# A two-block layer kernel: constants, first modulation, first normalisation, token turn and first projection made one stage

## The reference, cut to what matters

```
mod = silu(c) @ w_ada + b_ada                     # c: 1 x 1024, w_ada: 1024 x 6144
sh_m, sc_m, gt_m, sh_f, sc_f, gt_f = split(mod, 6)
u = layer_norm(x) * (1 + sc_m) + sh_m             # per token over 1024 columns
proj = u @ w_in                                   # w_in: 1024 x 2568
q, k, v, f_logit, xb, gb = split(proj, ...)       # 512 columns each; f_logit 8
...
```

## Time and profile before

| | |
|---|---|
| median of 3 runs | 2962.95 us |
| the profiled execution, own time | 2974.41 us |
| its span | 2972.7 us |
| PE / DVE / ACT / POOL busy over the span | 85% / 75% / 53% / 11% |
| end of the five stages in question | 211.98 us |
| first matmul of the projection | 74.12 us |

### The profile page before, as it was taken

One profiled execution on the slowest core, in us unless ns is written; L12 is line 12 of the kernel. 1 busy time (PEld: TensorE's weight loads), 2 busy tenths in 40 slices (PEclk: granted clock), 3 DMA queues, 4 the chain that ended last, 5 costly groups with the idle time before them and its releaser, 6 DMA issues. The chain is left out here.

```text
span 2972.7 us, 35763 instructions
## 1 busy us (share of the span) xinstructions
PE 2524.2 (85%) x12008; PEld 2035.5 (68%) x12008; DVE 2228.7 (75%) x2169; ACT 1572.1 (53%) x1443; POOL 337.3 (11%) x271
## 2 busy tenths in 40 slices
PE   2979774899982999778893999999999999999981
PEld 1862654677772888667773777777777777777761
DVE  4557874788775431678646899999999999999984
ACT  2214621676654431546421677777767777777760
POOL 1110100232320000000000011111111111111110
PEclk9989885999995999889985999999999999999995
DMA  5855222899974241010213899999999999999984
GB/s 185 284 192 195 26 105 111 325 350 367 372 269 159 89 127 48 1 67 19 71 73 128 323 367 367 365 365 368 366 364 364 369 362 370 364 367 366 367 306 163
DMA packets 247345, 731.59 MB, mean 246 GB/s; under 512 B 29388, under 2 KB 57307, under 8 KB 245023
## 3 DMA queue, kind: packets, MB, share of 16 engines
q1 hardware_dynamic: 223172, 645.64, 60.1%
q0 software_dynamic: 21792, 80.75, 7.1%
q10 hardware_dynamic: 2304, 4.20, 0.4%
HBM read 692.73 MB, written 39.39 MB: 246 GB/s over the span
## 5 line engine op out<-in xcount | busy, mean ns | idle before, releaser
L49 PE MATMUL psum_all<-sb_ring_r,sb_arena_r 128*128 128x512 f32 (+1 forms) x2464 | 951.7, 386 | 0.0
L155 DVE TENSOR_TENSOR sb_ring_r<-sb_ring,sb_hi_ring 128x2048 fp32r<-128x2048 f32 x285 | 647.5, 2288 | 174.7 <-ACT sb_hi_ring L146 169.6
L155 DVE TENSOR_TENSOR sb_ring_r<-sb_ring,sb_arena_r 128x2048 fp32r<-128x2048 f32 x258 | 582.2, 2285 | 36.9 <-ACT sb_arena_r L146 36.7
L146 ACT ACTIVATE sb_arena_r<-sb_ring 128x2048 fp32r<-128x2048 f32 x258 | 485.5, 1912 | 204.7 <-DMA sb_ring<-in_w_gu_dram 195.3
L146 ACT ACTIVATE sb_hi_ring<-sb_ring 128x2048 fp32r<-128x2048 f32 x285 | 542.7, 1915 | 81.0 <-DMA sb_ring<-in_w_gu_dram 37.8
L48 PE MATMUL psum_all<-sb_hi_ring,sb_arena_r 128*128 128x512 f32 (+1 forms) x1400 | 535.1, 382 | 36.3 <-DVE sb_ring_r L1635 18.3
L49 PEld LDWEIGHTS psum_all<-sb_ring_r,sb_arena_r 128*128 128x128 f32 x2464 | 472.5, 192 | 94.0
L50 PE MATMUL psum_all<-sb_hi_ring,sb_arena_r 128*128 128x512 f32 (+1 forms) x1400 | 530.1, 379 | 0.0
L48 PE MATMUL psum_all<-sb_arena_r 128*128 128x512 f32 x1080 | 436.2, 404 | 12.2 <-DVE sb_ring_r L155 7.0
L50 PE MATMUL psum_all<-sb_arena_r 128*128 128x512 f32 x1064 | 420.5, 395 | 0.0
L48 PEld LDWEIGHTS psum_all<-sb_hi_ring,sb_arena_r 128*128 128x128 f32 x1400 | 270.8, 193 | 94.2 <-DVE sb_ring_r L1635 18.5
(11 more groups left out here) (426 smaller groups left out, 3209.2 us busy)
## 6 DMA issues: line engine op xcount, KB each, us to landing
sb_ring<-in_w_gu_dram SPq DMA_DIRECT2D x272, 1024.0 KB, 7.1
sb_ring<-in_w_dn_dram SPq DMA_DIRECT2D x136, 1024.0 KB, 9.3
sb_ring<-in_w_e_gate_dram SPq DMA_DIRECT2D x36, 1024.0 KB, 7.7
sb_ring<-in_w_e_up_dram SPq DMA_DIRECT2D x36, 1024.0 KB, 7.3
sb_ring<-in_w_e_down_dram SPq DMA_DIRECT2D x36, 1024.0 KB, 8.0
sb_ring<-in_w_in_dram SPq DMA_DIRECT2D x27, 1024.0 KB, 5.8
sb_arena<-in_w_ada_dram POOLq DMA_DIRECT2D x16, 1024.0 KB, 5.7
sb_ring<-in_w_mod_dram SPq DMA_DIRECT2D x16, 1024.0 KB, 5.0
```

The costliest lines, as they stand in the source:

```text
L49: eng.matmul(out, a[0], b[1], start=False, stop=False)
L146: act.activation(s.hi[c % len(s.hi)], s.raw[c % len(s.raw)], ACT.Copy).then_inc(s.hi_made, 1)
L155: dve.tensor_tensor(s.lo[c % len(s.lo)], s.raw[c % len(s.raw)], s.hi[c % len(s.hi)].bitcast(F32), ALU.subtract).then_inc(s.lo_made, 1)
```

## The change

The five stages become one, `first_in`. What it does:

- ACT starts the bulk loads, as the first thing in its list: x in 4 parts of 512 KB, the 8 MB of `w_ada` for `sh1` and `sc1` into 8 places of their own, and the first two chunks of `w_in`. SP keeps the small row tiles, and starts the other 8 chunks once `sc1` is there.
- Of the 8 row blocks of a modulation piece, PE multiplies the first two (`direct_part`, 16 matmuls with one moving column), DVE accumulates the other six. The sum over partitions is made by 8 transposes on PE into two PSUM banks and one `tensor_reduce` on DVE, for all eight jobs.
- The statistics stand ahead of the accumulation in DVE's list, xn inside it.
- The token turn of block kk+2 stands ahead of the six matmuls of row block kk in the first chunk, so that turn and first chunk run together.
- The six later jobs get 48 loads of 512 KB in 6 slots (4 for the last 12) instead of 24 of 1 MB in 2; POOL's first two are started once the last `w_ada` part has landed, the next four after the turn.

The diff, cut to its core:

```diff
+class Modulation:
+    def __init__(self, nc, name, jobs, acc, pairs, slots, early):
...
+        total = KD * len(jobs)
+        first = total - 2 * (len(slots) - early)
+        first -= first % len(slots)
+        self.early, self.until = early, first
+        self.place = [c % len(slots) if c < first else early + (c - first) % (len(slots) - early) for c in range(total)]
...
+    def load(self, pool, c):
+        slot, n = self.place[c], self.use(c)
+        if n:
+            pool.wait_ge(self.s.acc, [b for b in range(c) if self.place[b] == slot][-1] + 1)
+        _, w, _, piece = self.jobs[c // KD][0:4]
+        src = w[0, c % KD * P:(c % KD + 1) * P, piece * D:(piece + 1) * D]
+        pool.dma_start(self.slots[slot], src).then_inc(self.landed[slot], 16)
...
+    def sum(self, k, pe, jobs):
+        for i in jobs:
+            pe.wait_ge(self.s.acc, KD * (i + 1))
+            if i >= 2:
+                pe.wait_ge(self.s.reduced, i - 1)
+            for kd in range(KD):
+                bank = k.psum[:, self.pairs[i % 2] + kd // 4, P * (kd % 4):P * (kd % 4) + P]
+                ins = pe.transpose(bank, self.acc[i % NACC][:, kd * P:(kd + 1) * P], k.ident[:])
+            ins.then_inc(self.s.summed, 1)
...
+            dve.wait_ge(self.s.summed, i + 1)
+            dve.tensor_reduce(total, pair, AX.X, ALU.add).then_inc(self.s.reduced, 1)
...
+def first_in(nc, k, a, xn, u, chunks, whole, ada, acc, later, held):
...
         @block.sync
         def _(sp):
...
-            sp.dma_start(k.x[:], a["x"].rearrange("o (t p) d -> p (o t) d", p=P)).then_inc(s.x_loaded, 16)
...
+            sp.wait_ge(s.put, 2)
+            for n in range(AHEAD, len(chunks)):
+                load_chunk(sp, k, ss, chunks[n]["src"], n)
...
         @block.gpsimd
...
+            pool.wait_ge(ada_landed[2 * NQ - 1], 16)
+            for c in range(len(mod.place)):
+                if c == mod.early:
+                    pool.wait_ge(s.turned, KD)
+                mod.load(pool, c)
 
         @block.tensor
         def _(pe):
+            def direct_part(i):
+                pe.wait_ge(ada_landed[NQ * i], 16)
+                chunk = ada[NQ * i].rearrange("p (k n) -> p k n", k=2)
+                for kd in range(KD):
+                    for kk in range(2):
+                        ins = pe.matmul(direct[i][:, kd:kd + 1], chunk[:, kk, kd * P:(kd + 1) * P], k.silu[:, kk:kk + 1],
+                                        start=kk == 0, stop=kk == 1)
+                ins.then_inc(s.direct, 1)
...
+            pe.wait_ge(s.silu, 1)
+            direct_part(0)
+            pe.wait_ge(s.normed, TT)
+            turn_x(0)
+            turn_x(1)
+            direct_part(1)
+            sum_up(0)
+            sum_up(1)
+            w = chunk_halves(pe, k, ss, 0, 256)
+            for kk in range(KD):
+                if kk + 2 < KD:
+                    turn_x(kk + 2)
+                pe.wait_ge(s.u_lo, kk + 1)
+                for i in range(2):
+                    ins = split3(pe, k.psum[:, i, :], [x[:, kk, i * P:(i + 1) * P] for x in w], [x[:, kk, :] for x in u],
+                                 kk == 0, kk == KD - 1)
...
         @block.scalar
         def _(act):
+            for t in range(TT):
+                act.dma_start(k.x[:, t, :], a["x"][0, t * P:(t + 1) * P, :]).then_inc(x_landed[t], 16)
+            for c in range(2 * NQ):
+                piece, q = c // NQ, c % NQ
+                src = a["w_ada"][0, q * 256:(q + 1) * 256, piece * D:(piece + 1) * D]
+                act.dma_start(ada[c].rearrange("p (k n) -> p k n", k=2),
+                              src.rearrange("(k p) n -> p k n", p=P)).then_inc(ada_landed[c], 16)
+            for n in range(AHEAD):
+                load_chunk(act, k, ss, chunks[n]["src"], n)
             act.wait_ge(s.copied, 1)
...
+            act.wait_ge(s.ready, 1)
+            act.activation(rstd, inv, ACT.Sqrt).then_inc(s.root, 1)
+            make_hi(act, k, ss, 0)
+            act.wait_ge(s.put, 2)
+            for i in range(KD):
+                act.wait_ge(s.turned, i + 1)
+                if i >= 2:
+                    act.wait_ge(s.u_lo, i - 1)
...
+            make_hi(act, k, ss, 1)
+            make_hi(act, k, ss, 2)
...
+                if n == held:
+                    act.wait_ge(mod.s.acc, mod.until)
...
         @block.vector
...
+            dve.wait_ge(s.silu, 1)
+            accumulate(0, 2)
+            dve.wait_ge(s.root, 1)
...
+            for kd in range(3, KD):
+                accumulate(0, kd)
+            add_bias(0)
+            accumulate(1, 2)
+            accumulate(1, 3)
+            put(0, "sh1", 0.0)
+            for kd in range(4, KD - 1):
+                accumulate(1, kd)
+            add_bias(1)
+            accumulate(1, KD - 1)
+            put(1, "sc1", 1.0)
+            make_lo(dve, k, ss, 0)
...
+            make_lo(dve, k, ss, 1)
+            make_lo(dve, k, ss, 2)
```

More of the change, by code:

```diff
@@ L332, in accumulate @@
+    def accumulate(self, k, dve, u):
+        for c in range(u * MOD_PER, min((u + 1) * MOD_PER, len(self.place))):
+            i, kd = c // KD, c % KD
+            acc, chunk, cond = self.acc[i % NACC], self.slots[self.place[c]], self.jobs[i][0]
+            scale = k.silu[:, KD * cond + kd:KD * cond + kd + 1]
+            dve.wait_ge(self.landed[self.place[c]], 16 * (self.use(c) + 1))
+            if kd == 0:
                 if i >= NACC:
@@ L405, in _ @@
         def _(sp):
-            m.load(sp)
+            for name, ap in rows:
+                first, n = COLUMNS[name]
+                sp.dma_start(row_tile[first:first + n, :], ap).then_inc(s.loaded, 16)
+            for i, b in enumerate(("b_ada", "b_mod_2")):
+                sp.dma_start(bias_tile[i * NBIAS:(i + 1) * NBIAS, :],
+                             a[b].rearrange("o (j p) -> (o j) p", p=P)).then_inc(s.loaded, 16)
+            sp.wait_ge(s.zero, 1)
+            pad = k.rpb_pad.rearrange("(o n) -> o n", o=1)
@@ L408, in _, with accumulate @@
         @block.vector
         def _(dve):
-            m.accumulate(k, dve, 0)
-            m.put(k, dve, range(len(jobs)))
-        @block.tensor
-        def _(pe):
-            m.sum(k, pe, range(len(jobs)))
+            link = chain(dve, s.chain)
+            def accumulate(i, kd):
+                c, kk = NQ * i + kd // 2, kd % 2
+                chunk = ada[c].rearrange("p (k n) -> p k n", k=2)[:, kk, :]
+                scale = k.silu[:, kd:kd + 1]
+                dve.wait_ge(ada_landed[c], 16)
+                if kd == 2:
+                    ins = dve.tensor_scalar(acc[i], chunk, scale, None, ALU.mult)
+                else:
+                    dve.wait_ge(s.acc, 6 * i + kd - 2)
+                    ins = dve.scalar_tensor_tensor(out=acc[i], in0=chunk, scalar=scale, in1=acc[i], op0=ALU.mult, op1=ALU.add)
+                ins.then_inc(s.acc, 1)
@@ L1368, in block_one_mixer @@
     cum = k.arena[0:NF, 22540:22540 + T]
-    normalise(nc, k, "n1", k.x, TT, D, xn, True, 1e-5)
     gate0 = 3 * DA + NH
-    turn(nc, k, "t1", xn, TT, KD, k.mod["sc1"], k.mod["sh1"], *u,
-         ahead=[column_chunk(a["w_in"][0], gate0 + 256 * h) for h in range(AHEAD)])
     def put_f(dst, j0, offset=0, scale=1.0):
```

459 lines of the change are left out of this document (179 added, 280 removed).

## The result

The changed kernel takes 2941.31 us (median of 4 runs, 2937.86 to 2945.33), the kernel before, in runs beside it, 2964.41. The ratio is 0.9929, with an interval of 0.9902 to 0.9957. Five more executions gave 0.9937 (0.9923 to 0.9950). The forecast was 2948, 6.7 us too high.

What follows compares the result with a forecast made beforehand. DMA, then DVE, in line bound the head, PE the chunks, the late modulation the tail. 10.1 - 3.9 + 2.1 + 6.0 = 14.3 us off the median 2962.95 gave 2948, range 2926 to 2957.

Steps and rivals of the forecast that it cites:

- The silu: Head: ACT held by its DMA issues until 158 pieces per engine are moved, so the silu is done at S = 30.0.
- the first of its two cases: Queue room from SP's issues before: two `w_in` chunks behind eleven 512 KB loads, about 134 pieces per engine outstanding.
- From silu to first matmul: Head, DVE's and PE's own work: first matmul 34 us after the silu, at 64.0 against 74.12, 10.1 us won.
- S + 19.2: Head, DVE: statistics, xn, the parts and a bias done 19.2 us after the silu's end, S.
- moving it is worth about nothing: Head: 4 of 16 parts, 5.6 us, taken off DVE, nearly given back by two reductions and PE's longer sums.
- Chunk 0: First projection chunk: 13.2 us before, 17.1 with 24 transposes among its matmuls, 3.9 us lost.
- Rival 2: Chunk 0: PE stays at half clock, 27.4 us instead of 17.1, 10 us less won, 2959; chance 0.09.
- Chunks 1 to 6: Projection: six chunks of 11.2, three sums of 1.3 and a 1.4 wait, 72.5 us, 2.1 won.
- Tail: From chunk 6 to the stage's end, late modulation: 44.1 us against 50.1, 6.0 won.
- Rival 1: Head: ACT's queue holds nothing, silu at S = 10.2, 19.8 us more won, 2928; chance 0.23.
- the last 0.01, for a stall: Chance of 0.01 left to a late clock or a stall behind the stage.
- Its own signs: ACT's `w_in` issues held until 21 to 29 us, first L48 at 62 to 66; wrong if late-modulation DVE waits for DMA.

Runs made afterwards that it cites:

- the runs with the silu at 14.93, 11.23 and 21.97: Against the changed kernel: `w_in` loads behind the square root, 2931.4 us; `w_ada` and `w_in` loads on SP, 2926.88; the first with `w_ada` in 2 KB pieces, 2935.88.

## Why the prediction was right

**The silu (forecast 30.0, end measured 27.4).** The mechanism is shown: ACT is held as SP is, which was an assumption, and taking the issues away moves everything by what they held. The size was off: the forecast let 158 pieces per engine, 10.3 MB, be moved at 393 GB/s before ACT was free. It was 9.27 MB, at 405 to 409 GB/s. The room in the queue, 130 in the forecast, was 146, counted by MB. The forecast had counted packets, and in the first of its two cases 139 of the 1317 are shorter than 512 bytes and no data. By MB its own two cases give 142 (4.83 MB) and 152 (1.71 MB), one on each side of 146. The Trainium skill's sentence that issuing is "usually small relative to the DMA itself" (DMA: Bandwidth & Descriptors, "Issuing engines are not separate DMA queues") doesn't hold here: 12.13 us for two issues, and 12.3 us of first L48 with them.

**From silu to first matmul (34, measured 33.0).** Counted from the silu's end, as the forecast did; from its start it is 33.2, and it stayed 33.2 in the runs with the silu at 14.93, 11.23 and 21.97. The sum is nearly right, and not for the reason given: 33 was forecast for a PE at full clock, but its 8 transposes took 1.95 and 1.97 us here, against 1.04 in the later sums, although the PEclk column says 1.00 for the stretch. It was the steps of DVE that were priced a little too dear, S + 19.2 for what was done at S + 18.1. One more step was wrong: "moving it is worth about nothing". It set the two reductions against the work taken off DVE, but those belong to the sums by transposes, which are there with or without the direct part. The direct part alone is worth 3.6 us at the first L48.

**Chunk 0 (17.1, measured 15.5).** The window of 16.8 us above takes in the wait ahead of chunk 1, which the forecast counted in the next term. PE's timeline:

```profile
65.62 0.60 PE L413 MATMUL psum_all<-sb_ident,sb_arena 128*128 128x128 f32 x4
...
67.46 0.60 PE L413 MATMUL psum_all<-sb_ident,sb_arena 128*128 128x128 f32 x4
...
77.38 0.50 PE L48 MATMUL psum_all<-sb_arena_r,sb_hi_ring 128*128 128x512 f32 x1 [1.48 <-DVE sb_ring_r L155]
```

The chunk runs from 60.37 to 75.9. From one group of four transposes to the next it is 1.84 us, of which six matmuls at 0.23 take 1.40. So a group costs 0.44 us and not the 0.66 forecast, which is how long one lasts in its row; it overlaps its neighbours. Six times 0.22 is 1.3 of the 1.6 us. PE waited 1.5 us ahead of chunk 1, for 1.4 forecast. Rival 2, the half clock through all of it, is out: from 64.7 us on the matmuls follow each other every 0.23 us, where the first ones stand 0.43 apart.

**Chunks 1 to 6 (72.5, measured 147.49 - 75.9 = 71.6).** The term that was off is the sum: a chunk with a sum behind it is 12.07 us, without 11.20, so the sum takes 0.87 and not 1.3. In the row it reads 1.04, as it overlaps its neighbours.

**Tail (44.1, measured 42.3).** DVE's groups in 60:190 (line, instruction, count, busy, mean ns, idle before):

```profile
L248 DVE TENSOR_SCALAR sb_rows<-sb_arena,sb_silu 128x1024 f32<-128x1024 f32 x4 | 3.0, 748 | 2.3 <-DMA sb_arena<-in_w_mod_dram 2.3
L251 DVE SCALAR_TENSOR_TENSOR sb_rows<-sb_arena,sb_silu,sb_rows 128x1024 f32<-128x1024 f32 x28 | 35.9, 1284 | 3.7 <-DMA sb_arena<-in_w_mod_dram 1.8
L273 DVE TENSOR_REDUCE sb_small<-psum_all 128x8 f32<-128x1024 f32 x6 | 7.3, 1217 | 0.0
```

DVE still waits 4.1 us for `w_mod`, twice the 2 us forecast, but a put is 1.4 us (1.22 and 0.17) and not 1.6. In the kernel before, DVE waited 35 us for these loads. The last chunk ends at 182.85, 35.4 us behind chunk 6, for 36.7 forecast: PE's own three chunks and two sums of 0.87 us are 35.3. What is left behind it takes 6.9 us, for 7.4.

**The sum.** 14.3 us were forecast and 22.2 measured: 2.6 at the silu, 1.0 behind it, 1.6 in chunk 0, 0.9 in chunks 1 to 6, 1.8 in the tail, all in one direction: each term had come out on the dear side, so their errors added up. Rival 1 was false as it stood, and shown to be open to whoever moves ten issues to SP. That the time came out 6.7 below the forecast and not 8 is the scatter behind the stage. The forecast gave 0.53 to faster and 0.40 to the same, with a bound at 0.5%; the interval of the ratio, 0.9902 to 0.9957, lies on both sides of 0.995, so these four executions don't decide between the two, and the five more, up to 0.9950, barely do. (Its parts for faster, 0.29 and 0.23, make 0.52; the last 0.01, for a stall, was counted there by mistake.)

**Its own signs.** The two `w_in` issues ended at 25.55 us, inside the 21 to 29 forecast. The first L48 at 60.37 lies below the 62 to 66. DVE rows that wait for DMA were named as a sign of being wrong, and they are there, 4.1 us in all; they cost nothing that shows, as PE is busy 105.43 of 105.70 us beside them.

## What to carry to other kernels

Count the pieces, not the bytes, that an engine's issue list puts ahead of its first computing instruction: here, once some 90 to 150 pieces per DMA engine were outstanding, the issuing engine itself stood still. Put bulk loads on an engine that computes nothing, or behind the small operation that everyone waits for. When two chains end close together (2.4 us here), shortening one gives only the difference, so move work in both.

## What was not expected of the hardware

The room of a queue depends on the size of the pieces: 94 with 4 KB, 112 with 2 KB, 146 with mostly 1 KB. The finer pieces cost little but the hold: by 13.3 us ACT's queue had moved 4.12 MB in pieces of 2 KB and 4.30 in pieces of 4 KB.

With two slots, POOL's loads of 512 KB came one per 3.1 us, so a slot's round was 6.2 us: 4.2 from issue to landing, 1.3 of DVE, the rest between them. Before's loads of 1 MB, also two at a time, landed in 5.7 us: half the bytes land only a quarter sooner. With six slots a load of the changed kernel took longer to land, 5.3 to 5.5 us, and yet DVE waited only 4.1 us in 48 loads.

The experts' stretch, the same code in every run, took 682.8 to 698.5 us. A difference of 10 us between two medians here may be nothing but that.
